# TensorE's lead of a few first-table steps behind each search of the expert layer, and the order of the first loads for the second table

## The chip, the cores and the metric

The kernel runs on one core of a Trainium2 chip. The metric is the device time of one execution in microseconds. Times in the rows are counted from the start of the profiled span.

## What is computed

The reference runs a two-layer latent/context transformer block and then a second block on 256 tokens of width 1024. The change lies in the expert ("PEER") layer, which is called for 512 tokens in layer 0 (latent and context tokens together) and for 256 tokens in layer 1. Cut to what matters:

```python
def peer(h, w_pq, sub_keys, u_tab, v_tab):
    q = (h @ w_pq).reshape(B, T, 8, 2, 64)
    s = einsum('bthcd,hckd->bthck', q, sub_keys)          # 128 keys per half
    top_s, top_i = top_k(s, 16)
    best_s, best_j = top_k(top_s[..., 0, :, None] + top_s[..., 1, None, :], 16)
    expert = i1 * 128 + i2                                 # one of 16384
    w = softmax(best_s)
    act = gelu(einsum('cd,ced->ce', h, u_tab[expert]))
    return einsum('ce,ced->cd', act * w, v_tab[expert])
```

## The kernel before

The two tables U and V (16384 x 1024 each) are not gathered for most tokens. They are run through densely, in 128 tiles `a` of 128 experts. In the **U phase** tile `a` gives gelu(U h) for all dense tokens (`u_product`, L944, three float32r products of high and low halves; in layer 1 some tiles are taken whole, `u_plain`, L919, and layer 1 adds a part sum, `u_sum`, L955). In the **V phase** (L1021 in layer 0, L1046 and L1048 in layer 1) the weighted activations are multiplied with the V tiles. For the first 128 tokens of layer 0 and the first 64 of layer 1, rows of U and V are gathered instead: GpSimd issues one indirect DMA for each of these rows (`u_row`, L2673, `v_row`, L2680), VectorE does the dot product (L2259) and, with V, the sum (L1831).

Beside the U phase runs the **search**, token block by token block (`t`, 128 tokens): TensorE makes four score groups (L982, `rt`), VectorE finds the best 16 of each (`choose`, L2111 and behind it) and ends with the weights of the block (`ww`, an L1823 on `area`). TensorE then transposes indices and weights (L644, `ti`), ScalarE copies them (L1618), VectorE and ScalarE build one-hot matrices for four tokens at a time (a **quad**; ScalarE's part is L1599 and L1604), TensorE multiplies them (L1000, `ow`), ScalarE copies the result (L1635), and GpSimd stores 16 tokens of it to `w_scratch` (L2753). The stored weights of 8 tiles at a time come back with `load_w` (L2763), the activations, stored by `store_g` (L2712), with `load_g` (L2775). Both are multiplied on VectorE (`weigh`) before the V product. VectorE's program has every gathered U row ahead of the first `weigh`.

The order around this is written by hand. Each engine has a generator `early()` that yields five times for each U tile, and calls `fill(n)` to go n **steps** on. On TensorE four steps of a tile hold a quarter of the products and the fifth holds none; a step with products is 6 matmuls of 384 columns in layer 0, 4 pairs in layer 1 (less in a plain tile). ScalarE makes the high half of tile a+2 (layer 0) or a+3 (layer 1) in a tile's first step (`high`, L1265); VectorE makes the low half in the fifth (`low`, an L1823 on `fr`); during the first part of layer 0's searches GpSimd makes the low half instead (L2695). `FILLS` holds the numbers: for layer 0 6 steps behind each score group, 10 for each half of the second selection, 14 for each third of the rest, 3 behind a quad; for layer 1 14, 25, 24 and 4. Counted so, layer 0's searches of t = 1, 2, 3 end at steps 144, 326 and 508 of 640, layer 1's of t = 0, 1 at steps 154 and 396. The block t = 0 of layer 0 is gathered whole and has no quads.

## Time and profile before

| | us |
|---|---|
| median of 3 runs | 3246.27 |
| lowest and highest of them | 3245.52, 3247.68 |
| the profiled execution, its own time | 3238.48 |
| its span | 3236.4 |
| layer 0: U phase about | 394 to 1064 |
| layer 0: V phase about | 1068 to 1592 |
| layer 1: U phase about | 1850 to 2265 |
| layer 1: V phase about | 2266 to 2560 |

TensorE is busy for 3009.5 us of the span (93%), VectorE for 2451.3 (76%), ScalarE for 1536.5 (47%), GpSimd for 942.6 (29%). In a row of the timeline the number in brackets is the idle time of the engine just ahead, and behind the arrow stands what ended it.

### The profile page before, as it was taken

To read this page: it belongs to the slowest core of one execution; us is meant where nothing else is said; L and a number is where in the kernel's file an instruction comes from. 1 tells how busy PE (TensorE), PEld (TensorE's weight loads), DVE (VectorE), ACT (ScalarE), POOL (GpSimd) and SP (SyncE) were. 2 spreads that over 40 slices of the span, in tenths; PEclk is the share of its full clock that TensorE was granted. 3 is DMA by queue.
4 is the path that set the end of the run, shared out by engine and by line. 5 is a ranking of instruction groups with operands and counts; after the bars stand their busy time and mean duration, and the time that the engine had idled before them with its cause. 6 is when DMAs were issued, how large, how long until landed. Compare 5 with 4: busy or idle time off the path is not lost.

```text
span 3236.4 us, 49042 instructions
## 1 busy us (share of the span) xinstructions
PE 3009.5 (93%) x19164; PEld 2657.7 (82%) x19164; DVE 2451.3 (76%) x4976; ACT 1536.5 (47%) x2895; POOL 942.6 (29%) x835
## 2 busy tenths in 40 slices
PE   6998999999999999999979899899999999988898
PEld 4656799989999888888765899888998899755898
DVE  2696588897888688888758678897999866668654
ACT  3455335737557333333444547496555543232543
POOL 0000046565656344344000024454685200000000
PEclk9999999999999999999998999999999999967899
DMA  7384347969789999999527568899999867501444
GB/s 233 97 283 157 127 159 273 341 242 315 271 286 339 370 371 353 381 357 368 174 96 256 182 227 315 278 351 361 380 400 400 325 207 247 158 33 47 155 142 132
DMA packets 352934, 824.41 MB, mean 255 GB/s; under 512 B 20256, under 2 KB 216384, under 8 KB 332608
## 3 DMA queue, kind: packets, MB, share of 16 engines
q1 hardware_dynamic: 257216, 469.79, 41.8%
q0 software_dynamic: 93120, 347.17, 29.3%
q10 hardware_dynamic: 2368, 4.32, 0.4%
q8 instruction: 152, 2.49, 0.3%
q14 instruction: 78, 0.64, 0.1%
HBM read 747.76 MB, written 73.40 MB: 254 GB/s over the span
## 4 chain that ended last, share of the span: by engine, by line
PE 65%; DVE 22%; DMA 6%; ACT 4%; issue 2%; POOL 1%; DVEq 0%; SPq 0%; ACTq 0%; POOLq 0%
PE ps L1021 16%; PE ps L944 16%; PE ps L639 13%; DVE fr L1823 5%; DVE area L1831 4%; DVE area L1823 3%; DMA ring<-in_peer_v 3%; PE ps L1000 3%; PE ps L1109 2%; PE ps L717 2%; PE ps L1101 2%; PE ps L873 2%; DVE plain L2259 1%; ACT fr L1265 1%; PE ps L919 1%
## 5 line engine op out<-in xcount | busy, mean ns | idle before, releaser
L1823 DVE TENSOR_TENSOR fr<-ring,fr 128x1024 fp32r<-128x1024 f32 x641 | 781.7, 1222 | 473.3 <-ACT fr L1265 470.5
L1265 ACT CAST fr<-ring 128x1024 fp32r<-128x1024 f32 x677 | 703.7, 1045 | 566.5 <-PE ps L1021 323.5
L944 PE MATMUL ps<-fr 128*128 128x384 f32 (+1 forms) x4784 | 851.0, 331 | 14.2 <-DVE fr L1823 14.1
L944 PEld LDWEIGHTS ps<-fr 128*128 128x128 f32 x4784 | 789.2, 191 | 19.5 <-DVE fr L1823 17.1
L1021 PE MATMUL ps<-fr 128*128 128x512 f32 x2304 | 523.9, 390 | 4.4 <-DVE fr L1823 4.4
L1021 PEld LDWEIGHTS ps<-fr 128*128 128x128 f32 x2304 | 433.4, 188 | 94.8 <-ACT area L1582 4.7
L639 PE MATMUL ps<-fr 128*128 128x256 f32 (+1 forms) x2928 | 415.3, 304 | 26.2 <-DVE fr L1823 26.2
L639 PEld LDWEIGHTS ps<-fr 128*128 128x128 f32 x2928 | 389.1, 193 | 52.3 <-DVE fr L1823 32.5
L2680 POOL DMA_INDIRECT plain<-in_peer_v,area x192 | 284.9, 1484 | 259.6 <-DVE area L1831 167.0
L1046 PE MATMUL ps<-fr 128*128 128x384 f32 x1024 | 297.6, 362 | 12.9 <-DVE fr L1823 12.4
L2712 POOL DMA_DIRECT2D g_scratch<-area x224 | 127.0, 567 | 581.1 <-ACT area L1582 540.9
L1048 PE MATMUL ps<-fr 128*128 128x192 f32 x1024 | 256.4, 250 | 0.0
L1831 DVE SCALAR_TENSOR_TENSOR area<-plain,area 128x1024 f32<-128x1024 f32 x190 | 243.1, 1279 | 1.0
L1582 ACT ACTIVATE area<-ps 128x384 f32<-128x384 f32 (+1 forms) x256 | 105.7, 413 | 278.8 <-PE ps L944 235.5
L2673 POOL DMA_INDIRECT plain<-in_peer_u,area x128 | 196.1, 1532 | 120.4 <-DVE plain L2259 97.9
L1046 PEld LDWEIGHTS ps<-fr 128*128 128x128 f32 x1024 | 192.1, 188 | 20.9 <-DVE fr L1823 19.9
L2695 POOL TENSOR_TENSOR fr<-ring,fr 128x1024 fp32r<-128x1024 f32 x36 | 91.4, 2539 | 392.0 <-ACT fr L1265 391.6
L1048 PEld LDWEIGHTS ps<-fr 128*128 128x128 f32 x1024 | 195.5, 191 | 0.0
L1823 DVE TENSOR_TENSOR area<-area 128x384 f32<-128x384 f32 (+9 forms) x391 | 183.5, 478 | 7.6 <-DMA area<-w_scratch 5.3
L2259 DVE SCALAR_TENSOR_TENSOR plain<-plain,area 128x1024 f32<-128x1024 f32 x128 | 157.6, 1237 | 15.8 <-DMA plain<-in_peer_u,area 15.8
L1000 PE MATMUL ps<-area 128*128 128x128 f32 x1152 | 154.1, 277 | 10.9 <-DVE area L1828 5.0
L1545 ACT CAST fr<-area 128x384 fp32r<-128x384 f32 (+1 forms) x256 | 110.0, 430 | 107.6 <-DVE area L1823 107.2
(228 smaller groups left out, 3990.5 us busy)
## 6 DMA issues: line engine op xcount, KB each, us to landing
ring<-in_peer_uT SPq DMA_DIRECT2D x128, 1024.0 KB, 6.2
ring<-in_peer_v SPq DMA_DIRECT2D x128, 1024.0 KB, 10.0
ring<-in_w_mod SPq DMA_DIRECT2D x48, 1024.0 KB, 5.3
w_scratch<-acc POOLq DMA_DIRECT2D x36, 1024.0 KB, 8.4
g_scratch<-area POOLq DMA_DIRECT2D x128, 192.0 KB, 5.2
area<-g_scratch POOLq DMA_DIRECT2D x64, 384.0 KB, 8.8
area<-w_scratch POOLq DMA_DIRECT2D x16, 1536.0 KB, 10.0
ring<-in_w_ada SPq DMA_DIRECT2D x24, 1024.0 KB, 5.1
```

The source lines that it names most:

```text
L639: ins = e.matmul(o, lhs, rhs, start=(n == 0), stop=(n == len(pairs) - 1))
L944: ins = e.matmul(o[:, 0:width], pairs[m][0], pairs[m][1], start=(m == 0), stop=(l == 0 and m == last), skip_group_check=l == 1)
L1000: ins = e.matmul(o[:, 128 * j:128 * j + 128], b.OH[:, half, 0, j, :], b.OH[:, half, 1, j, :], start=True, stop=True)
L1021: ins = e.matmul(M.PS[2 * tb + half][:, :], x[:, r, 128 * tb:128 * tb + 128], v[:, c, 512 * half:512 * half + 512], start=(a == 0 and (r, ...
L1046: e.matmul(M.PS[m][:, b.first:T + D], v[:, 0, 128 * m:128 * m + 128], x[:, :, 0:D], start=(a == 0), stop=False, skip_group_check=True)
L1048: ins = e.matmul(M.PS[m][:, b.first:T], v[:, 1, 128 * m:128 * m + 128], x[:, 0, 0:D], start=False, stop=False, skip_group_check=True)
L1265: e.copy(hi, x).then_inc(act.after(("high", name)), 1)
L1823: return e.tensor_tensor(o, a, b, op).then_inc(dve.after(*labels), 1)
L1831: return e.scalar_tensor_tensor(out=o, in0=a, scalar=s, in1=b, op0=op0, op1=op1).then_inc(dve.after(*labels), 1)
L2259: e.scalar_tensor_tensor(out=x, in0=x, scalar=1.0, in1=b.hx, op0=M_, op1=M_, accum_out=b.dot[:, k:k + 1]).then_inc(dve.after(("urow", l, k ...
L2673: e.indirect_dma_start(b.u_rows[k % U_ROWS], None, A[f"peer_u{l}"], bass.IndirectOffsetOnAxis(ap=b.idx[:, k:k + 1], axis=0)).then_inc(M.u_ ...
L2680: e.indirect_dma_start(b.v_rows[k % n], None, A[f"peer_v{l}"], bass.IndirectOffsetOnAxis(ap=b.idx[:, k:k + 1], axis=0)).then_inc(M.v_row_i ...
```

## The change

On TensorE, once a search with quads behind it has been covered, four more U steps are issued ahead of the wait for the weights and the transposes (`early_steps`); the next search takes four fewer behind its first score group. ScalarE does the same with three steps, in layer 1 alone. VectorE's and GpSimd's step counts stay as they are. On GpSimd the first `load_w` moves five steps up in layer 0, ahead of one gather and one store; in layer 1 the first `load_g` moves five steps down instead, and `load_w` stays at its step. The second `load_w` goes behind the second `load_g` and five more steps. The first gathers of V rows, eight and six at once before, go out one by one, one for each tile of the V phase.

```diff
+AHEAD_STEPS = {"pe": (4, 4), "act": (0, 3)}
...
-        quad = 0
+        quad = early_steps = 0
...
-                fill(fill_a)
+                fill(fill_a - (early_steps if h4 == 0 else 0))
...
+            early_steps = AHEAD_STEPS["pe"][l]
+            fill(early_steps)
             w.wait_ge(dve, ("ww", l, t))
...
-            fill(4 * fill_a + 2 * fill_b)
+            fill(4 * fill_a + 2 * fill_b - early_steps)
...
+            early_steps = AHEAD_STEPS["act"][l]
+            fill(early_steps)
             w.wait_ge(pe, ("ti", l, t))
...
-        fill(5)
+        fill(5 + 5 * l)
         w.wait_ge(pe, ("ow", l, D // 4 - 1))
         w.wait_ge(dve, ("oh", l, D // 4 - 1))
         load_g(KEPT[l] // 2 + 0)
-        fill(5)
         for i in range(2):
             w.wait_ge(M.w_stored[i], ("w", l, nst - 2 + i))
         load_w(0)
+        fill(5)
+        load_g(KEPT[l] // 2 + 1)
+        fill(5)
+        load_w(1)
         fill(3)
-        load_g(KEPT[l] // 2 + 1)
-        load_w(1)
-        fill(5)
         load_g(KEPT[l] // 2 + 2)
         load_g(KEPT[l] // 2 + 3)
...
-        for k in range(len(b.v_rows)):
-            v_row(k)
+        v_row(0)
         for a in range(128):
+            if a + 1 < len(b.v_rows):
+                v_row(a + 1)
```

TensorE at the end of layer 0's search of t = 1, before (the rows on `con,area` are the transposes of indices and weights):

```order
L944 MATMUL ps7<-fr 128x384 [waits act_done,dve_done]
L944 MATMUL ps7<-fr 128x384 x23
L644 MATMUL ps0<-con,area 128x128 [waits act_done,dve_done]
L644 MATMUL ps0<-con,area 128x128 x2
L944 MATMUL ps1<-fr 128x384 [waits act_done]
```

The same place in the changed kernel:

```order
L946 MATMUL ps6<-fr 128x384 x23
L946 MATMUL ps7<-fr 128x384 [waits act_done,dve_done]
L946 MATMUL ps7<-fr 128x384 x17
L646 MATMUL ps0<-con,area 128x128 [waits act_done,dve_done]
L646 MATMUL ps0<-con,area 128x128 x2
L946 MATMUL ps7<-fr 128x384 x6
```

Eighteen matmuls of the next tile, three steps with products and one empty one, now stand ahead of the transposes.

TensorE at the start of layer 0's search of t = 3, before (the rows on `area` are score groups):

```order
L982 MATMUL ps0<-area 128x128 x4
L944 MATMUL ps7<-fr 128x384 x18
L944 MATMUL ps1<-fr 128x384 [waits dve_done]
L944 MATMUL ps1<-fr 128x384 x11
L982 MATMUL ps2<-area 128x128 x4
```

And in the changed kernel:

```order
L984 MATMUL ps0<-area 128x128 x4
L946 MATMUL ps1<-fr 128x384 [waits dve_done]
L946 MATMUL ps1<-fr 128x384 x11
L984 MATMUL ps2<-area 128x128 x4
```

Between the first and the second score group 12 matmuls are left of 30.

GpSimd at the end of layer 0's U phase, before, from its last store of expert weights on:

```order
L2753 DMA w_scratch<-acc 128x16x128 [waits act_done]
L2673 DMA plain<-in_peer_u,area 128x1024 [waits dve_done]
L2673 DMA area<-in_peer_u,area 128x1024 [waits dve_done]
L2712 DMA g_scratch<-area 128x384 [waits act_done]
L2775 DMA area<-g_scratch 128x2x384 [waits g_stored1,g_stored0,pe_done]
L2673 DMA area<-in_peer_u,area 128x1024 [waits dve_done]
L2712 DMA g_scratch<-area 128x384 [waits act_done]
L2763 DMA area<-w_scratch 128x3072 [waits w_stored1,w_stored0]
```

And in the changed kernel, from the same store on:

```order
L2759 DMA w_scratch<-acc 128x16x128 [waits act_done]
L2679 DMA plain<-in_peer_u,area 128x1024 [waits dve_done]
L2679 DMA area<-in_peer_u,area 128x1024 [waits dve_done]
L2718 DMA g_scratch<-area 128x384 [waits act_done]
L2781 DMA area<-g_scratch 128x2x384 [waits g_stored1,g_stored0,pe_done]
L2769 DMA area<-w_scratch 128x3072 [waits w_stored1,w_stored0]
L2679 DMA area<-in_peer_u,area 128x1024 [waits dve_done]
L2718 DMA g_scratch<-area 128x384 [waits act_done]
```

The load of the first weights has gone ahead of the last gathered U row and of one store.

## Rows read from the trace of the kernel before

**Rows 1.** Page, part 4: chain that ended last, by engine.

```profile
PE 65%; DVE 22%; DMA 6%; ACT 4%; issue 2%; POOL 1%; DVEq 0%; SPq 0%; ACTq 0%; POOLq 0%
```

**Rows 2.** Waits of TensorE, 395 to 1070: us in total, times, longest.

```profile
PE ps L644 <- DVE area L1823: 12.0, 3, 5.4
```

**Rows 3.** Timeline of TensorE, layer 0: start, us, line, count, idle ahead.

```profile
529.29 0.90 PE L644 MATMUL ps<-con,area 128*128 128x128 f32 x3 [3.28 <-DVE area L1823]
529.84 14.14 PE L944 MATMUL ps<-fr 128*128 128x384 f32 x66
...
718.16 1.32 PE L944 MATMUL ps<-fr 128*128 128x384 f32 x6 [1.61 <-DVE fr L1823]
724.86 0.90 PE L644 MATMUL ps<-con,area 128*128 128x128 f32 x3 [5.37 <-DVE area L1823]
...
741.12 1.13 PE L1000 MATMUL ps<-area 128*128 128x128 f32 x8 [2.02 <-DVE plain L2259]
...
914.17 3.42 PE L944 MATMUL ps<-fr 128*128 128x384 f32 x18 [1.48 <-DVE fr L1823]
920.98 0.90 PE L644 MATMUL ps<-con,area 128*128 128x128 f32 x3 [3.39 <-DVE area L1823]
921.53 12.98 PE L944 MATMUL ps<-fr 128*128 128x384 f32 x66
935.40 1.13 PE L1000 MATMUL ps<-area 128*128 128x128 f32 x8 [0.88 <-ACT area L1604]
```

**Rows 4.** Windows: us, busy of PE, PEld, DVE, ACT, POOL, PEclk, DMA share, GB/s.

```profile
530.00:534.00 4.00, 4.00 (x14) 4.00 (x14) 3.28 (x5) 1.97 (x4) 3.31 (x3) 0.50 0.80 199
```

**Rows 5.** Timeline of VectorE, first selection of layer 0's searches.

```profile
654.90 3.12 DVE L1823 TENSOR_TENSOR fr<-ring,fr 128x1024 fp32r<-128x1024 f32 x1
...
672.53 0.89 DVE L2111 MAX8 area<-ps 128x8 f32<-128x128 f32 x4 [0.69 <-PE ps L982]
...
870.86 0.89 DVE L2111 MAX8 area<-ps 128x8 f32<-128x128 f32 x4 [1.66 <-PE ps L982]
```

**Rows 6.** Timeline of GpSimd beside the first of these.

```profile
654.52 2.42 POOL L2695 TENSOR_TENSOR fr<-ring,fr 128x1024 fp32r<-128x1024 f32 x1
```

**Rows 7.** Timeline of TensorE, layer 0's last U products and first V product.

```profile
1042.62 21.05 PE L944 MATMUL ps<-fr 128*128 128x384 f32 x120
1068.05 7.12 PE L1021 MATMUL ps<-fr 128*128 128x512 f32 x24 [4.37 <-DVE fr L1823]
```

**Rows 8.** Timeline of GpSimd there: last store, last gather, first weights' load.

```profile
1043.78 1.21 POOL L2753 DMA_DIRECT2D w_scratch<-acc  x1 [0.40 <-ACT acc L1635]
...
1050.21 1.55 POOL L2673 DMA_INDIRECT area<-in_peer_u,area  x1 [0.30 <-issue]
...
1052.61 0.55 POOL L2763 DMA_DIRECT2D area<-w_scratch  x1
```

**Rows 9.** Timeline of VectorE there: last gathered U row, first weigh.

```profile
1059.20 1.22 DVE L2259 SCALAR_TENSOR_TENSOR area<-area 128x1024 f32<-128x1024 f32 x1 [1.49 <-DMA area<-in_peer_u,area]
...
1065.74 0.56 DVE L1823 TENSOR_TENSOR area<-area 128x384 f32<-128x384 f32 x1 [5.30 <-DMA area<-w_scratch]
```

**Rows 10.** Timeline of TensorE, layer 1: ends of both searches, first quads, a part sum.

```profile
1939.05 0.55 PE L644 MATMUL ps<-con,area 128*128 128x128 f32 x3 [2.54 <-DVE area L1823]
...
2096.49 0.90 PE L644 MATMUL ps<-con,area 128*128 128x128 f32 x3 [7.02 <-DVE area L1823]
...
2113.09 1.13 PE L1000 MATMUL ps<-area 128*128 128x128 f32 x8 [1.86 <-ACT area L1604]
...
2133.88 0.35 PE L955 MATMUL ps<-area_r 128*128 128x192 f32 x1 [0.35 <-ACT area_r L1566]
```

**Rows 11.** Timeline of VectorE, layer 1, t = 1: the last score group.

```profile
2028.41 0.89 DVE L2111 MAX8 area<-ps 128x8 f32<-128x128 f32 x4 [3.02 <-PE ps L982]
```

**Rows 12.** Timeline of GpSimd, layer 1: first weights' load.

```profile
2223.86 0.60 POOL L2763 DMA_DIRECT2D area<-w_scratch  x1 [7.18 <-DMA w_scratch<-acc]
```

**Rows 13.** Windows, layer 1, tail of the U phase and first V tiles.

```profile
2165.00:2360.00 195.00, 186.65 (x1300) 182.66 (x1301) 173.72 (x272) 127.69 (x248) 114.36 (x67) 0.99 0.98 371
```

More of the change, by code:

```diff
@@ L1605, in one_hot @@
                     act.after(("oh", l, quad)), 1)
-        quad = 0
+        quad = early_steps = 0
         for t in range(T // 128):
-            fill(4 * fill_a + 2 * fill_b)
+            fill(4 * fill_a + 2 * fill_b - early_steps)
             w.wait_ge(dve, ("wsub", l, t))
```

## The prediction

> **What bounds the kernel now.** I read the page first: by the chain that ended last the kernel is TensorE for 65% and VectorE for 22% [rows 1]. Then the waits of TensorE over layer 0's U phase: almost all that it waits there stands ahead of the transposes at the ends of the searches, 12.0 us in three waits, for an instruction of VectorE [rows 2]. The timeline puts them: 3.28 us at t = 1, 1.61 + 5.37 at t = 2, 1.48 + 3.39 at t = 3 [rows 3]. So a search lasts as long as VectorE's selection, and from the transposes to the next search TensorE is without a gap, except for the first quad of a block (2.02 and 0.88 us) [rows 3]. Layer 1 has the same picture, with 2.54 and 7.02 us, and 1.86 us at a first quad [rows 10].
>
> The idle time has a price behind it. In 530 to 534, right behind the first wait, the granted clock is 0.50 (1.2 GHz) [rows 4]; 66 matmuls take 14.14 us there and 12.98 us behind the search of t = 3 [rows 3], where the last 120 of the phase take 21.05, 0.175 each [rows 7], so that 66 would take 11.6.
>
> **A trap first.** Four steps ahead of a wait don't shorten anything by themselves: they are taken from the next search, at whose end TensorE idles again. Search time is VectorE's; the stretch from transposes to next search keeps its number of products. What can be gained is (a) time that VectorE waits for TensorE within a search, (b) slow clock behind the idle time, (c) the waits at first quads, where ScalarE starts its one-hots only once TensorE has finished the tile.
>
> **Layer 0, t = 1.** Four steps are 18 matmuls, 3.16 us, into a wait of 3.28 [rows 3]; their low halves stand ahead of `ww` in VectorE's program, since TensorE uses a tile six steps after VectorE's turn for it. The transposes keep their time. The idle time is gone, and with it the slow clock: 14.14 - 11.6 = **-2.6**. Bounds: 0 if the clock falls all the same, -2.6. I take -2.6, since nothing is left to wait for.
>
> **t = 2.** The second to fourth score groups come 18 matmuls (3.1 us) earlier. VectorE waited for the last one for only 0.69 us [rows 5], so the search gets **-0.6**. The first quad's 2.02 us [rows 3] go: with four steps ahead the tile that ScalarE waits for is finished long before, **-2.0**. The idle time of the search, 6.98 less 0.6, stays but falls apart: VectorE's last low halves come every 6 us against 4.2 us of products for a tile, so about 2 us stand ahead of each of the last two tiles and 2.5 ahead of the transposes. Whether the clock falls then is open: between 0 and the 1.4 to 2.6 us that it costs at the other two searches. I take half, **-1.1**.
>
> **t = 3.** VectorE waits 1.66 us for each of three score groups (one of three like rows [rows 5]), 4.98 in all; they come 18 matmuls earlier, so the search is shortened by **-3.1**. The first quad's wait goes, **-0.9** [rows 3]. Idle time falls from 4.87 to about 1.7, so the slow clock goes: 12.98 - 11.6 = **-1.4**. By the count of steps one more with products falls ahead of the last quad, **+1.0**. Sum of layer 0 up to its last quad: -10.7.
>
> **Between quads.** The low half of a tile now sometimes stands behind the one-hots of the same quad on VectorE, where TensorE waited for nothing of its own. There the half is ready about 2 us before TensorE gets to it by my count of steps, so 0. Bounds: -1 and the rival below.
>
> **From the last quad to V.** This is a chain: product, copy, store, load of the weights, `weigh`, ScalarE's and VectorE's halves. It takes from 1042.6 to 1068.05, and 21.05 us of U products lie beside it [rows 7]. Four steps fewer are left, so products cover only 16.8 of it: of what the lead wins at t = 3's end nothing is won here, and TensorE idles about 9 us. The load moves up: at most from 1052.61 to where the gather was issued, 1050.21, so -2.4 [rows 8]. But the last gathered row goes behind it. Before, that row had landed by 1059.2 and the weights (1.5 MB) by 1065.7 [rows 9], 6.5 us later in one queue where landings kept the order of issue. Turned round, the row comes last, near 1065.1 (one store fewer is ahead), then 1.22 us of VectorE for it, then `weigh` at 1066.3 instead of 1065.74: **+0.5**. Bounds -2.4 (the row isn't held up) and +2. I take the queue's order, since both rows are from it. The longer idle time makes the V phase start slow for longer: its first 24 products took 7.12 us [rows 7], some 1.5 more than 0.175 x 512/384 each gives; I add **+0.7**, bounds 0 and +2. V rows one by one, and the second weights later, cost nothing: they are due six and eight V tiles on, 4 us each. Layer 0: -10.7 + 0.5 + 0.7 = -9.5.
>
> **Layer 1.** At t = 0 the transposes keep their time, 2 us of products go into 2.54 [rows 10], and the slow clock was not there; nothing. The search of t = 1 starts three steps with products shorter, 1.8 us; VectorE waited longer than that for the last score group (3.02 [rows 11]), and its later waits for high halves move with TensorE: **-1.8**. First quad of t = 1: of 1.86 us 0.2 is left, since ScalarE is one step behind TensorE instead of level: **-1.7**; at t = 0 the part sum then waits on ScalarE, **+0.4**. The 7.02 us become about 5, and the slow clock behind them stays. Between quads the three engines are nearly level; one part sum in four waited 0.35 [rows 10], now two will, within what VectorE leaves idle: 0, bounds -3 and +3.5. GpSimd's 7.18 us wait for the last store [rows 12] stands at the same step and holds the same gathers; the V phase starts a fixed time after the last quad. Of -3.1 I take four fifths, **-2.5**, since DMA is at 0.98 there [rows 13].
>
> **The sum.** -9.5 - 2.5 = -12.0. Against that the whole search meets GpSimd's low halves elsewhere: one low half on VectorE took 3.12 us [rows 5] beside a subtraction on GpSimd that ran until 656.94 [rows 6], against 1.22 for the others. There are a handful of such meetings in each search, some 2 us each; they can fall either way, and I add 1. That is -11.0: the profiled execution's 3238.5 would be 3227.5, and as the median of the runs lies 7.8 above that execution, 3246.3 - 11 = **3235**.
>
> The Trainium skill (SBUF — State Buffer, section "Who interferes with whom") says that a VectorE instruction with two inputs in SBUF and a GpSimd instruction that reads SBUF don't share: the later one is fully blocked. By that rule the trace agrees (3.12 ends 1.1 us after the subtraction's end). It speaks against counting the 3.1 us at t = 3 as safe, and is the third rival.
>
> **The rivals.**
> 1. *Nothing but the first quads.* VectorE's selection turns out to be paced by its own work, and the clock falls behind the scattered idle time as before. For it: TensorE's idle time only changes place. Against it: three waits of 1.66 on score groups. Left are -2.9 and -1.3 at first quads and -0.6 in the search of t = 2, with +1.2 at the V start: -3.6, **3242**. Chance 0.25.
> 2. *Slower: low halves behind the one-hots.* With TensorE four steps on, a low half issued behind a quad's one-hots comes too late once in every five quads. It decides if VectorE, held by a gathered row, is more than about 2 us late there. Such a wait was 1.48 to 1.61 at search ends [rows 3]; 19 times in layer 0 and 10 in layer 1 at 0.8 is +23, less 11: **3258**. For it: VectorE's rows wait for gathers near the end. Against it: no such wait in the quads before. Chance 0.1.
> 3. *Collisions.* One or two more blocked instructions in each of the three searches, 2 us each, +6 on the forecast: **3241**. Chance 0.15.
> 4. *More.* The last gathered row isn't held up by the weights, and the clock stays up at t = 2: -2.9 and -1.1, **3231**. Chance 0.15.
>
> The forecast itself has 0.35.
>
> **How the numbers follow.** A measurement tells 0.2% here, 6.5 us, so faster is below 3239.8. The forecast is nearly all in that, the fourth rival too, the third by a third; the first is within. Faster 0.54, same 0.35, slower 0.11 (the second rival and a little of the third). The range takes the forecast, the first, third and fourth rivals with their bounds: 3228 to 3247.
>
> **What would show it.** In the changed profile: the wait at the first transposes under 0.5 us and PEclk at 1.00 behind it; score groups of t = 3 without waits of 1.66 on VectorE and that search 3 us shorter; no waits at first quads of layer 0; an idle TensorE of about 9 us ahead of the first V product, with a gathered row, not the weights, as the last thing that VectorE waits for. Waits of TensorE for an L1823 on `fr` within the quads, or a V start more than 28 us after the last quad, would prove me wrong.

## The result, and the profile after

| | before | after |
|---|---|---|
| median of 7 runs, us | 3244.16 | 3224.98 |
| lowest and highest | 3236.31, 3247.68 | 3215.46, 3229.71 |
| ratio, with 95% interval | | 0.9949 (0.9938 to 0.9961) |
| span of the profiled execution | 3236.4 | 3222.9 |

The change makes the kernel 0.5% faster: by the ratio 16.5 us, with an interval from 12.7 to 20.1. The forecast was 11 us and 3235; the time lies below its range, which began at 3228. Of all executions of all kernels below, one of six_steps' ten took 4776.6 us at a mean granted clock of 0.56, where the other nine had 0.93 to 0.96; it is left out of its ratio.

Line numbers of TensorE's part are two to four higher in the changed kernel (L944 is L946, L644 is L646, L982 is L984, L1000 is L1004, L1021 is L1025, L955 is L957), those of ScalarE four to six (L1566 is L1570, L1604 is L1608, L1635 is L1641), those of VectorE and GpSimd six (L1823 is L1829, L2111 is L2117, L2673 is L2679).

First the timeline of TensorE in layer 0, the rows that answer to [rows 3] (start, us, line, count, in brackets the idle time just ahead and what ended it):

```profile
532.18 0.55 PE L646 MATMUL ps<-con,area 128*128 128x128 f32 x3 [0.16 <-DVE area L1829]
532.48 11.71 PE L946 MATMUL ps<-fr 128*128 128x384 f32 x66
544.04 1.05 PE L1004 MATMUL ps<-area 128*128 128x128 f32 x8
...
716.38 4.46 PE L946 MATMUL ps<-fr 128*128 128x384 f32 x24 [1.61 <-DVE fr L1829]
723.08 0.55 PE L646 MATMUL ps<-con,area 128*128 128x128 f32 x3 [2.24 <-DVE area L1829]
723.38 12.75 PE L946 MATMUL ps<-fr 128*128 128x384 f32 x72
735.97 1.05 PE L1004 MATMUL ps<-area 128*128 128x128 f32 x8
...
909.56 2.37 PE L946 MATMUL ps<-fr 128*128 128x384 f32 x12 [0.36 <-DVE fr L1829]
911.77 0.49 PE L646 MATMUL ps<-con,area 128*128 128x128 f32 x3
...
915.00 9.64 PE L946 MATMUL ps<-fr 128*128 128x384 f32 x54 [0.65 <-DVE fr L1829]
```

Of 3.28, 5.37 and 3.39 us ahead of the three transposes 0.16, 2.24 and nothing are left, and the waits at the first quads (2.02 and 0.88) are gone. New is a wait of 0.65 us for a low half between the transposes and the first quad of t = 3. The slow clock behind the first wait is gone too: 66 products take 11.71 us where they took 14.14. The windows behind the three transposes and behind layer 0's V start say so (column by column: busy time of PE, PEld, DVE, ACT, POOL, then the granted clock, the DMA share and GB/s):

```profile
532.50:536.50 4.00, 4.00 (x26) 4.00 (x24) 3.63 (x5) 3.30 (x6) 3.67 (x3) 1.00 0.78 192
723.40:727.40 4.00, 4.00 (x26) 4.00 (x24) 4.00 (x6) 1.98 (x4) 2.66 (x3) 1.00 0.97 292
912.00:916.00 4.00, 3.35 (x21) 3.03 (x20) 4.00 (x6) 3.40 (x6) 2.76 (x2) 1.00 0.52 152
1056.30:1060.30 4.00, 4.00 (x11) 3.13 (x12) 2.34 (x4) 0.79 (x3) 3.10 (x3) 0.57 0.98 392
```

Where [rows 4] had 0.50, the granted clock is 1.00 behind all three searches; only behind the longest idle stretch, ahead of V, it is still at its lower level for most of the window.

Then the way from layer 0's last quad to V, TensorE's rows against [rows 7], GpSimd's (last store, load of the first weights, last gather) against [rows 8], VectorE's against [rows 9]:

```profile
1031.22 12.74 PE L946 MATMUL ps<-fr 128*128 128x384 f32 x72
1045.83 6.03 PE L946 MATMUL ps<-fr 128*128 128x384 f32 x24 [1.87 <-DVE fr L1829]
1056.25 44.04 PE L1025 MATMUL ps<-fr 128*128 128x512 f32 x186 [4.39 <-DVE fr L1829]
```

```profile
1032.39 1.21 POOL L2759 DMA_DIRECT2D w_scratch<-acc  x1 [2.87 <-ACT acc L1641]
...
1040.04 0.57 POOL L2769 DMA_DIRECT2D area<-w_scratch  x1 [1.24 <-DMA w_scratch<-acc]
1040.91 0.99 POOL L2679 DMA_INDIRECT area<-in_peer_u,area  x1 [0.30 <-issue]
```

```profile
1052.79 1.23 DVE L2265 SCALAR_TENSOR_TENSOR area<-area 128x1024 f32<-128x1024 f32 x1 [5.88 <-DMA area<-in_peer_u,area]
1053.94 0.08 DVE L2265 DVE_READ_ACCUMULATOR area<-area 128x1 f32 x1
1053.94 0.55 DVE L1829 TENSOR_TENSOR area<-area 128x384 f32<-128x384 f32 x1
```

The last thing that VectorE waits for is now a gathered row, which was issued 0.87 us behind the load and landed 11.9 us after its issue (before, ahead of the load, 9.0 us). `weigh` follows with no wait for the weights. TensorE stands idle for 6.3 us ahead of V (1.87 and 4.39), not for the 9 that the prediction named as a sign: the last 24 products take 6.03 us at a granted clock of 0.72, where 24 take 4.2 at 1.00.

On VectorE the two rows that answer to [rows 5], the low half beside GpSimd's subtraction and the one wait for a score group that is left of t = 3's three:

```profile
655.01 2.57 DVE L1829 TENSOR_TENSOR fr<-ring,fr 128x1024 fp32r<-128x1024 f32 x1
```

```profile
861.46 0.89 DVE L2117 MAX8 area<-ps 128x8 f32<-128x128 f32 x4 [1.66 <-PE ps L984]
```

Between the quads of layer 0 TensorE waits for nothing; before, one quad of t = 3 had waited for a one-hot of VectorE:

```profile
990.75 1.16 PE L1000 MATMUL ps<-area 128*128 128x128 f32 x8 [1.17 <-DVE area L1828]
```

In layer 1 the transposes at 2081.71 wait 2.62 us and the products ahead of them 2.12, where 7.02 stood [rows 10]. But between the quads of t = 1 there are more waits than before. The waits of TensorE and of ScalarE there, first of the kernel before (2113 to 2209), then of the changed one (2098 to 2197); columns: us in total, times, longest:

```profile
PE ps L1000 <- DVE area L1828: 2.6, 6, 0.4
PE ps L955 <- ACT area_r L1566: 2.0, 6, 0.3
...
ACT acc L1635 <- PE ps L1000: 1.1, 6, 0.2
```

```profile
PE ps L957 <- ACT area_r L1570: 6.2, 12, 0.7
...
ACT acc L1641 <- PE ps L1004: 4.6, 12, 0.6
```

**All stages at once.** From the timeline of TensorE the start of each stage's first matmul can be read; the stages between them are in this table, in us, with two of the experiments below beside them. Within layer 0's U phase up to the last quad, stages with the same program repeat from kernel to kernel within 0.15 us, but for the quads of t = 3 (105.9 to 106.7 in the nine kernels with four steps). Other stages scatter more: the first row takes 392.3 to 401.2 us over all fourteen profiles, the stretch from layer 1's last quad to V 53.8 to 58.8. So a difference of a microsecond in the former can be read from a single profile, where the medians tell 4.

| stage | before | after | l0_only | act_level |
|---|---|---|---|---|
| start to first score group, layer 0 | 392.26 | 395.19 | 397.57 | 397.38 |
| to transposes t = 1 | 137.03 | 136.99 | 137.02 | 137.01 |
| to first quad | 14.54 | 11.86 | 11.85 | 11.86 |
| quads, to search t = 2 | 109.07 | 108.97 | 108.98 | 108.97 |
| search t = 2 | 71.96 | 70.07 | 70.07 | 70.09 |
| to first quad | 16.26 | 12.89 | 12.89 | 12.89 |
| quads, to search t = 3 | 109.07 | 107.93 | 107.94 | 107.93 |
| search t = 3 | 70.79 | 67.87 | 67.88 | 67.86 |
| to first quad | 14.42 | 12.71 | 12.71 | 12.73 |
| quads, to the last one | 106.41 | 105.93 | 105.91 | 106.26 |
| last quad to V | 26.24 | 25.84 | 27.97 | 24.78 |
| V phase, projections of layer 1 | 782.29 | 779.63 | 779.13 | 783.91 |
| layer 1: search t = 0 | 88.71 | 88.81 | 89.48 | 88.79 |
| to first quad | 13.86 | 13.88 | 15.05 | 13.80 |
| quads of t = 0 | 49.31 | 50.72 | 49.32 | 48.08 |
| search t = 1 | 94.27 | 92.42 | 94.27 | 92.42 |
| to first quad | 16.60 | 16.22 | 16.50 | 17.14 |
| quads of t = 1 | 96.12 | 98.48 | 96.22 | 93.98 |
| last quad to V | 57.15 | 57.28 | 54.36 | 53.92 |
| V start to the end | 970.04 | 969.21 | 969.28 | 972.00 |

Layer 0 from its first score group to V is 14.7 us shorter (675.79 and 661.06), layer 1 from its first score group to V 1.8 us longer (416.02 and 417.81). The 2.9 us at the top, where the program is the same, and the 2.7 of the "V phase, projections" row are within such scatter and not shown to be work of the change. The granted clock differs there: in a stretch of layer 1's first projections it is 0.63 before (1604 to 1622) and 0.81 after (1592 to 1610).

### The profile page after: what moved, and what is told of

It is laid out like the page before. It is cut to its first block, busy times and chain, and to the rows that moved or that the text cites. A ratio compares the mean times of both kernels' runs of the same rounds, so it can differ in the third digit from the quotient of the medians.

```text
span 3222.9 us, 48984 instructions
## 1 busy us (share of the span) xinstructions
PE 3010.5 (93%) x19164; PEld 2659.3 (83%) x19164; DVE 2447.6 (76%) x4976; ACT 1533.6 (48%) x2895; POOL 960.5 (30%) x835
## 4 chain that ended last, share of the span: by engine, by line
PE 67%; DVE 21%; DMA 5%; ACT 4%; issue 2%; POOL 1%; DVEq 0%; SPq 0%; POOLq 0%; ACTq 0%
PE ps L946 16%; PE ps L1025 16%; PE ps L641 14%; DVE fr L1829 5%; DVE area L1837 4%; PE ps L1004 3%; DVE area L1829 3%; DMA ring<-in_peer_v 3%; PE ps L719 2%; PE ps L1113 2%; PE ps L1105 2%; PE ps L875 2%; ACT fr L1269 1%; PE ps L921 1%; DVE acc L1829 1%
## 5 line engine op out<-in xcount | busy, mean ns | idle before, releaser
L1829 DVE TENSOR_TENSOR fr<-ring,fr 128x1024 fp32r<-128x1024 f32 x641 | 779.8, 1219 | 458.6 <-ACT fr L1269 454.8
L946 PE MATMUL ps<-fr 128*128 128x384 f32 (+1 forms) x4784 | 851.5, 331 | 19.8 <-DVE fr L1829 19.8
L946 PEld LDWEIGHTS ps<-fr 128*128 128x128 f32 x4784 | 787.9, 191 | 26.3 <-DVE fr L1829 24.2
L1025 PE MATMUL ps<-fr 128*128 128x512 f32 x2304 | 524.1, 390 | 4.4 <-DVE fr L1829 4.4
L1025 PEld LDWEIGHTS ps<-fr 128*128 128x128 f32 x2304 | 433.5, 188 | 94.9 <-ACT area L1586 4.7
L2686 POOL DMA_INDIRECT plain<-in_peer_v,area x192 | 299.7, 1561 | 251.9 <-DVE area L1837 170.1
L2679 POOL DMA_INDIRECT plain<-in_peer_u,area x128 | 194.3, 1518 | 124.2 <-DVE plain L2265 104.7
L1829 DVE TENSOR_TENSOR area<-area 128x384 f32<-128x384 f32 (+9 forms) x391 | 182.7, 475 | 5.6 <-DMA area<-g_scratch 3.8
L1004 PE MATMUL ps<-area 128*128 128x128 f32 x1152 | 152.8, 275 | 2.0 <-ACT area L1608 2.0
```

The costliest lines, as they stand in the source:

```text
L946: ins = e.matmul(o[:, 0:width], pairs[m][0], pairs[m][1], start=(m == 0), stop=(l == 0 and m == last), skip_group_check=l == 1)
L1004: ins = e.matmul(o[:, 128 * j:128 * j + 128], b.OH[:, half, 0, j, :], b.OH[:, half, 1, j, :], start=True, stop=True)
L1025: ins = e.matmul(M.PS[2 * tb + half][:, :], x[:, r, 128 * tb:128 * tb + 128], v[:, c, 512 * half:512 * half + 512], start=(a == 0 and (r, ...
L1829: return e.tensor_tensor(o, a, b, op).then_inc(dve.after(*labels), 1)
L2679: e.indirect_dma_start(b.u_rows[k % U_ROWS], None, A[f"peer_u{l}"], bass.IndirectOffsetOnAxis(ap=b.idx[:, k:k + 1], axis=0)).then_inc(M.u_ ...
L2686: e.indirect_dma_start(b.v_rows[k % n], None, A[f"peer_v{l}"], bass.IndirectOffsetOnAxis(ap=b.idx[:, k:k + 1], axis=0)).then_inc(M.v_row_i ...
```

## The experiments

Two questions stand: is the gain all layer 0's, and why does layer 1 lose what its shorter search wins? The times are compared with runs of the kernel before on the same chip. All kernels take the changed kernel and alter the numbers of `AHEAD_STEPS` or GpSimd's order.

### Which part of the change does what

**l0_only**: the steps ahead in layer 0 alone.

```diff
-AHEAD_STEPS = {"pe": (4, 4), "act": (0, 3)}
+AHEAD_STEPS = {"pe": (4, 0), "act": (0, 0)}
```

> Four steps ahead in layer 0 alone (the pair of numbers (4, 0) for TensorE, (0, 0) for ScalarE), GpSimd's new order in both layers. Theory A (from comparing the two traces by stages: layer 0's U phase is 14.7 us shorter, layer 1 from its first score group to its V start is 1.8 us longer): this kernel is 2 us faster than the changed one, 18 to 21 us faster than the kernel before, and its stretches between quads in layer 1 are 49.3 and 96.1 us again, as in the kernel before. Theory B (as forecast: both layers gain, 2.5 us of it in layer 1): it is 2 to 3 us slower than the changed one, and the search of t = 1 in layer 1 lasts 94.3 us again while the stretches between quads don't change.

Measured: 3226.5 us, ratio 0.9950 (0.9936 to 0.9965), which is 16.2 us. The quads of layer 1 are back at 49.32 and 96.22 us, the search of t = 1 at 94.27. Layer 0 gives the same 14.3 us up to its last quad. As a time of the whole it can't be told from the change, and A's 18 to 21 us are not reached. By its stages A's mechanism holds: from the first quad of t = 0 in layer 1 to the last one of t = 1 it takes 256.3 us, as before, against 257.8. But layer 0's V starts 27.97 us after the last quad against 25.84, with the same program: there the gathered row landed 14.0 us after its issue in place of 11.9.

**l1_only**: the steps ahead in layer 1 alone.

```diff
-AHEAD_STEPS = {"pe": (4, 4), "act": (0, 3)}
+AHEAD_STEPS = {"pe": (0, 4), "act": (0, 3)}
```

> Steps ahead in layer 1 alone ((0, 4) for TensorE, (0, 3) for ScalarE), GpSimd's new order in both layers. Theory A: the search of t = 1 in layer 1 is 1.9 us shorter and the stretches between quads are 1.4 and 2.4 us longer; with nothing from layer 0 the time is that of the kernel before or up to 3 us more. Theory B: 2.5 to 4 us faster than the kernel before, since the longer stretches between quads in the changed kernel's profile were chance.

Measured: 3244.0 us, ratio 1.0008 (0.9997 to 1.0018): nothing won. The search of t = 1 is 92.50 us, the quads are 50.83 and 98.34. The longer quads of the changed kernel were no chance. Theory B, at least 2.5 us faster, falls: the interval ends at 1.0 us faster.

**gpsimd_only**: no steps ahead, GpSimd's new order alone.

```diff
-AHEAD_STEPS = {"pe": (4, 4), "act": (0, 3)}
+AHEAD_STEPS = {"pe": (0, 0), "act": (0, 0)}
```

> No steps ahead in either layer, only GpSimd's new order (the first two weight loads moved, V rows issued one by one). Theory A (the weights load earlier but the last gathered row is held up behind them, so nothing is won): within 1 us of the kernel before; V starts 25 to 26 us after the last quad of layer 0, and the last thing VectorE waits for there is a gathered row. Theory B (the order on GpSimd is where the unexpected part of the gain came from, since the changed kernel won 8 us more than forecast by the medians): 3 to 8 us faster than the kernel before, with the gain in a V phase or at its start.

Measured: 3245.8 us, ratio 1.0009 (1.0000 to 1.0018). No gain, so theory B falls; by the ratio it is 2.9 us slower (0 to 5.8), where A had at most 1. From layer 0's last quad to V it took 28.76 us, 2.5 more than before and beyond what theory A gave, since the gathered row came 15.2 us after its issue (14.6 in l1_only). VectorE's row for it:

```profile
1074.29 1.22 DVE L2265 SCALAR_TENSOR_TENSOR area<-area 128x1024 f32<-128x1024 f32 x1 [8.71 <-DMA area<-in_peer_u,area]
```

In layer 1 the same order made the way from the last quad to V 53.77 us instead of 57.15, so that in these two profiles the two nearly cancel (but see order_by_layer for the second).

**tensor_only**: the steps ahead with GpSimd's old order.

```diff
-        fill(5 + 5 * l)
+        fill(5)
...
         load_g(KEPT[l] // 2 + 0)
+        fill(5)
         for i in range(2):
             w.wait_ge(M.w_stored[i], ("w", l, nst - 2 + i))
         load_w(0)
-        fill(5)
-        load_g(KEPT[l] // 2 + 1)
-        fill(5)
-        load_w(1)
         fill(3)
+        load_g(KEPT[l] // 2 + 1)
+        load_w(1)
+        fill(5)
...
-        v_row(0)
+        for k in range(len(b.v_rows)):
+            v_row(k)
         for a in range(128):
-            if a + 1 < len(b.v_rows):
-                v_row(a + 1)
```

> The steps ahead as in the change, (4, 4) and (0, 3), with GpSimd's order as in the kernel before. Theory A: as fast as the changed kernel within 1.5 us (16 to 19 us faster than the kernel before); at the last quad of layer 0 the weights are what VectorE waits for last, 1 to 2 us after the row has come, and V starts 24.5 to 26 us after the last quad. Theory B: 3 to 8 us slower than the changed kernel, because the steps alone give what was forecast for them.

Measured: 3221.4 us, ratio 0.9942 (0.9927 to 0.9957). The whole gain is there without GpSimd's part, and V starts 24.76 us after the last quad. The gather of the last row and the load behind it on GpSimd, then what VectorE waits for:

```profile
1039.09 1.00 POOL L2679 DMA_INDIRECT area<-in_peer_u,area  x1 [0.30 <-issue]
1040.67 0.55 POOL L2769 DMA_DIRECT2D area<-w_scratch  x1
```

```profile
1047.70 1.23 DVE L2265 SCALAR_TENSOR_TENSOR area<-area 128x1024 f32<-128x1024 f32 x1 [0.51 <-DMA area<-in_peer_u,area]
1052.86 0.56 DVE L1829 TENSOR_TENSOR area<-area 128x384 f32<-128x384 f32 x1 [3.92 <-DMA area<-w_scratch]
```

With the row first, it lands 8.6 us after its issue, and the weights, loaded 0.6 us later than in the changed kernel, are weighed 1.1 us sooner (1052.86 against 1053.94). A had the time, the V start and the weights as the last wait right; the row came 5.2 us ahead of the weights, not 1 to 2.

**order_by_layer**: steps in layer 0 alone; GpSimd's old order of the first loads in layer 0, the new one in layer 1, as `if l == 0:` with the old lines and `else:` with the new ones. The V rows still go out one by one.

> Four steps ahead in layer 0, none in layer 1; GpSimd's order as in the kernel before in layer 0 and as in the change in layer 1. Theory A (the gain is layer 0's steps, 14.3 us up to its last quad in every profile that has them; GpSimd's new order costs 1 to 2.5 us at layer 0's V start and wins about 3 us from layer 1's last quad to its V start): the stretch from the last quad to V in layer 0 is 24.8 us, in layer 1 53.8 to 54.4 us, and the kernel is 17 to 21 us faster than before, 1 to 4 us faster than the changed one. Theory B (the differences of GpSimd's order are chance of landings): layer 1's stretch is 55.9 to 57.2 us again and the time is the changed kernel's.

Measured: 3222.2 us, ratio 0.9945 (0.9927 to 0.9963), within A's 17 to 21 us at 17.8. Layer 0's stretch from last quad to V was 24.73, as A had it. Layer 1's was 56.11, theory B's value, which A had at 53.8 to 54.4: over all the profiles with GpSimd's new order in layer 1 that stretch took 53.8 to 58.8 us, with the old one 57.15 (before) and 55.87 (tensor_only). So the 3 us that I read from two profiles are not shown; the stretch hangs on something that differs between executions.

### Why layer 1 loses between its quads

In the changed kernel ScalarE is three steps ahead and TensorE four, so that ScalarE stands one step further behind than before. The next four kernels alter these numbers in layer 1; all have GpSimd's order by layer, as order_by_layer.

**act_level**: as order_by_layer, with both engines four steps ahead in layer 1:

```diff
-AHEAD_STEPS = {"pe": (4, 0), "act": (0, 0)}
+AHEAD_STEPS = {"pe": (4, 4), "act": (0, 4)}
```

> Four steps ahead in both layers, and four for ScalarE in layer 1 in place of three, so that ScalarE stands to TensorE between quads as it did before; GpSimd's order by layer as in order_by_layer. Theory A (ScalarE is the busiest engine between quads in layer 1; being one step further behind TensorE it and TensorE wait for each other, 0.7 us per part sum): layer 1's stretches between quads fall from 50.8 and 98.4 to about 48.7 and 95 us, with the search of t = 1 still 92.4: 2 to 3 us faster than order_by_layer. Theory B (the stretches are longer because VectorE or the transfers fall behind when TensorE is ahead): they stay at 50.8 and 98.4 us, and the kernel is 2 us slower than order_by_layer.

**act_two**: (4, 4) and (0, 2).

> As act_level, (4, 4) for TensorE, but two steps ahead for ScalarE in layer 1 in place of four. Theory A (each step that ScalarE stands further behind TensorE costs in layer 1 between quads: with four there the stretches are 48.1 and 94.0 us, with three 50.8 and 98.4): with two they are 51 to 54 and 100 to 104 us. Theory B (three steps were only an unlucky meeting of the two orders, and the distance as such costs nothing): with two they are 48 to 49 and 94 to 96 us.

**act_five**: (4, 4) and (0, 5).

> As act_level, but five steps ahead for ScalarE in layer 1 in place of four: ScalarE is one step nearer to TensorE than in the kernel before. Theory A (the nearer the better, until ScalarE waits for products): the waits of TensorE for part sums fall from 0.7 us, the stretches between quads are 47 to 48 and 92.5 to 94 us, and the kernel is as fast as act_level or 1 to 2 us faster. Theory B (level is the optimum, since a cast of a step that TensorE has not done holds up the one-hots behind it): they are 49 to 51 and 95 to 98 us, and the kernel is 2 to 4 us slower than act_level.

**three_l1**: (4, 3) and (0, 3).

> Three steps ahead in layer 1 on both TensorE and ScalarE, else as act_level. Theory A (what matters is that both have the same number): the stretches between quads are 48 to 49 and 94 to 95 us, the search of t = 1 is 92.4 to 93.5 us. Theory B (what matters is that TensorE and ScalarE meet at certain steps, and three is a bad number for ScalarE): they are 50 to 51 and 97 to 99 us, as with (4, 3).

Measured for the four:

| TensorE's, ScalarE's steps in layer 1 | quads t = 0 | quads t = 1 | search t = 1 | time, ratio |
|---|---|---|---|---|
| 0, 0 (order_by_layer) | 49.34 | 96.12 | 94.31 | 3222.2, 0.9945 |
| 4, 2 (act_two) | 54.64 | 107.27 | 92.49 | 3240.4, one run |
| 4, 3 (the change) | 50.72 | 98.48 | 92.42 | 3225.0, 0.9949 |
| 4, 4 (act_level) | 48.08 | 93.98 | 92.42 | 3215.7, 0.9919 (0.9901 to 0.9937) |
| 4, 5 (act_five) | 48.94 | 93.60 | 92.49 | 3225.1, 0.9931 (0.9908 to 0.9954) |
| 3, 3 (three_l1) | 49.38 | 93.75 | 93.04 | 3222.2, one run |

Theory A had the direction each time and the size too small: 48.7 and 95 us for act_level, at most 54 and 104 for act_two. The distance of ScalarE behind TensorE sets the price: from level to one step behind 2.6 and 4.5 us, one more step another 3.9 and 8.8. Level with three steps gives what level with four gives at t = 1, so it isn't the number three. Level with four is also shorter than level with none, by 1.3 and 2.1 us. Why isn't tested; VectorE's waits for ScalarE's high halves between the quads of t = 1 go the same way, 1.3 us in all against 6.7 in order_by_layer (7.2 in the changed kernel, 14.9 in act_two). The waits between the quads of t = 1, of act_level (2103 to 2197) and of act_two (2105 to 2213):

```profile
ACT acc L1641 <- PE ps L1004: 1.3, 1, 1.3
...
PE ps L957 <- ACT area_r L1570: 4.0, 6, 0.7
```

```profile
PE ps L957 <- ACT area_r L1570: 13.5, 19, 1.3
...
ACT acc L1641 <- PE ps L1004: 12.9, 24, 0.8
```

Read with the two programs, and with the sizes in the table, it is a wait in both directions: TensorE's part sum waits for ScalarE's cast (L1570), which stands one step late in ScalarE's program, and ScalarE's copy (L1641) then waits for the quad's products (L1004), which stand behind that part sum in TensorE's. Each such pair is time in which ScalarE, the busiest engine here, does nothing. The windows of the stretch, of the kernel before, the changed one and act_level:

```profile
2113.09:2209.21 96.12, 91.48 (x673) 88.14 (x674) 89.28 (x164) 94.20 (x229) 49.69 (x43) 1.00 0.96 351
```

```profile
2097.93:2196.41 98.48, 91.89 (x670) 87.50 (x670) 91.28 (x167) 93.07 (x229) 47.23 (x43) 1.00 0.96 347
```

```profile
2103.00:2197.00 94.00, 89.66 (x672) 87.56 (x671) 91.41 (x165) 92.23 (x228) 48.97 (x43) 1.00 0.98 358
```

ScalarE is busy for 94.20 of 96.12, for 93.07 of 98.48, and for 92.23 of 94.00 us. By the ratios act_level is about 8 us faster than order_by_layer, with intervals that overlap; by the stages from layer 1's first quad to its last it is 4.8 (251.6 against 256.4), where A had 2 to 3. Five steps for ScalarE give nothing more between the quads than four (142.54 us in the two stretches against 142.06), nor do they cost what B had there. By its ratio act_five is 4 us slower than act_level, and the intervals overlap widely, so the time doesn't decide between the two theories.

### How far ahead

**two_steps** and **six_steps**: as order_by_layer, with two and with six steps in layer 0. **seven_l1**: as act_level, with seven steps on both engines in layer 1.

```diff
-AHEAD_STEPS = {"pe": (4, 0), "act": (0, 0)}
+AHEAD_STEPS = {"pe": (2, 0), "act": (0, 0)}
```

> Two steps ahead in layer 0 in place of four, else as order_by_layer. Theory A (idle time of 1.5 to 2 us or more ahead of the transposes lets the clock fall, and part of the waits is left): at t = 1 the wait is 1.2 to 3.3 us and the stretch from the transposes to the first quad is 14.5 us, as without steps; up to the last quad 6 to 9 us are won of the 14.3. Theory B (the slow clock comes of long waits alone): that stretch is 11.9 us, and 11 us or more are won.

Measured: 3228.0 us in one run; 11.15 us are won up to the last quad of layer 0, theory B's side. TensorE's rows at the ends of the three searches:

```profile
531.68 0.55 PE L646 MATMUL ps<-con,area 128*128 128x128 f32 x3 [2.23 <-DVE area L1829]
531.98 11.69 PE L946 MATMUL ps<-fr 128*128 128x384 f32 x66
...
723.39 0.55 PE L646 MATMUL ps<-con,area 128*128 128x128 f32 x3 [3.30 <-DVE area L1829]
723.70 11.72 PE L946 MATMUL ps<-fr 128*128 128x384 f32 x66
...
906.33 4.46 PE L946 MATMUL ps<-fr 128*128 128x384 f32 x24 [1.48 <-DVE fr L1829]
913.14 0.90 PE L646 MATMUL ps<-con,area 128*128 128x128 f32 x3 [2.35 <-DVE area L1829]
913.69 14.00 PE L946 MATMUL ps<-fr 128*128 128x384 f32 x72
```

Behind a wait of 2.23 us and behind one of 3.30 the clock stays up (66 products in 11.7 us). Behind 1.48 and 2.35 us it is at its lower level, 0.50 from 913 to 916, and 1.00 from 916.5 on (72 in 14.00). So neither theory has the clock right: a wait of 3.30 us passed without it and one of 2.35 did not. Two steps out of four already bring back 11 of the 14.3 us, because a full clock at t = 1 and t = 2 is won by both.

> Six steps ahead in layer 0 in place of four, else as order_by_layer. Theory A (the search of t = 3 still holds about 1.9 us of waits of VectorE for score groups, that of t = 2 3.8 us of waits of TensorE; at t = 1 nothing is left): t = 1 loses up to 2 us at the transposes and has them back in the next search; t = 3's search is 1 to 2 us shorter; all in all 0 to 2 us faster than order_by_layer. Theory B (the transposes are then late for the first quad of each block, or VectorE's low halves fall behind): 2 to 5 us slower, with waits at the first quads or within the quads of layer 0.

Measured: 3236.2 us, ratio 0.9981 (0.9968 to 0.9994): 12 us slower than with four by the ratios (8.1 up to layer 0's last quad by the stages), more than B gave, and at another place. The search of t = 2 takes 77.39 us instead of 70.07. Its first rows on VectorE, and GpSimd's beside them:

```profile
655.71 0.89 DVE L2117 MAX8 area<-ps 128x8 f32<-128x128 f32 x4 [3.98 <-PE ps L984]
656.52 5.81 DVE L1829 TENSOR_TENSOR fr<-ring,fr 128x1024 fp32r<-128x1024 f32 x1
```

```profile
656.02 2.35 POOL L2701 TENSOR_TENSOR fr<-ring,fr 128x1024 fp32r<-128x1024 f32 x1
658.30 0.56 POOL L2718 DMA_DIRECT2D g_scratch<-area  x1
658.88 2.35 POOL L2701 TENSOR_TENSOR fr<-ring,fr 128x1024 fp32r<-128x1024 f32 x1
```

A low half on VectorE that takes 1.22 us elsewhere takes 5.81: it begins inside one of GpSimd's subtractions and ends 1.1 us after the end of the second (661.23). It is the low half that TensorE, now six steps on, needs next, and TensorE stands still for 6.16 us:

```profile
662.38 8.13 PE L946 MATMUL ps<-fr 128*128 128x384 f32 x30 [6.16 <-DVE fr L1829]
```

The 30 products behind it take 8.13 us in place of 5.49 in order_by_layer, and the granted clock of 658 to 669 is 0.54. With four steps (order_by_layer) the wait at this place is 1.14 us. This is the third rival's mechanism: it decides at six steps and not at four; five weren't run. The last products of that search wait for low halves as well, 1.59 and 1.50 us, and the transposes stand behind them.

> Seven steps ahead in layer 1 on both engines, else as act_level. In act_level TensorE still waits 2.1 and 5.2 us at the end of layer 1's search of t = 1. Theory A (the remaining idle time takes three more steps): the wait ahead of the transposes falls from 5.2 to about 2.5 us, and the kernel is 1 to 3 us faster than act_level. Theory B (as with six in layer 0, the products at the search's end then stand ahead of the transposes and wait for low halves that VectorE has not done): the searches of layer 1 are 2 us or more longer and the kernel is 2 to 8 us slower.

Measured: 3224.3 us, ratio 0.9934 (0.9918 to 0.9951). The wait ahead of the transposes of t = 1 is gone and that search is 0.6 us shorter (91.87), so A was right that the wait shrinks; it had 2.5 us left. B's longer searches are not there. But from the transposes to the first quad it takes 19.60 us instead of 17.14, and the quads take 50.00 and 95.54: the part sums behind the transposes wait 1.82 and 1.14 us for ScalarE. Over layer 1 it is 7.5 us longer than act_level (415.65 and 408.13), at a place that neither theory named.

## Why the prediction was too small

Three steps of it failed. Layer 0's terms add up to -9.5, and the profiles show -14.7. Layer 1's term "between quads ... 0" was +1.4 and +2.4. And the 7.8 us that were added because "the median of the runs lies 7.8 above that execution" were not there in the changed kernel.

Point by point, as the prediction's steps have them; forecast and measurement in us.

| step | forecast | measured |
|---|---|---|
| layer 0, t = 1: idle time filled, clock up | -2.6 | -2.7 |
| t = 2: search | -0.6 | -1.9 |
| t = 2: first quad and clock | -3.1 | -3.4, with 6 products more in it |
| t = 2: quads | 0 | -1.1 |
| t = 3: search | -3.1 | -2.9 |
| t = 3: first quad and clock | -2.3 | -1.7 |
| t = 3: quads | +1.0 | -0.5, with 6 products more and a wait of 1.17 gone |
| last quad to V, V start | +1.2 | -0.4 |
| layer 0 | -9.5 | -14.7, with 0.1 in the quads of t = 1 |
| layer 1: search t = 0, its first quad | +0.4 | +0.1 |
| quads of t = 0 | 0 | +1.4 |
| search t = 1 | -1.8 | -1.9 |
| its first quad | -1.7 | -0.4, with 4 products more |
| quads of t = 1 | 0 | +2.4 |
| last quad to V | 0 | +0.1 |
| layer 1 (forecast at four fifths) | -2.5 | +1.8 |

**Layer 0.** The mechanisms held at nearly every place: the transposes of t = 1 stand where they stood, TensorE's clock stays at 1.00 behind the searches, the first quads don't wait, VectorE's waits of 1.66 us for score groups fell from three to one, and that search is 2.9 us shorter. Four terms were mis-sized. *The clock at t = 2* was taken at half; it stayed up, also with two steps, and 66 products fell from 13.68 to about 11.7 us. *The search of t = 2*: VectorE's work on the fourth score group begins 1.12 us sooner in the search, by the 0.69 us of the wait and by a low half that a subtraction of GpSimd held up for less (2.57 us in place of 3.12). The other 0.8 is a conversion behind it (L2148, now L2154): it took 1.50 us from 677.40 and now 0.73 from 676.39, in both kernels ending 0.15 us behind the end of a subtraction of GpSimd (678.76, 676.97). I had put +1 on such meetings over the whole; here they fell the other way, and with six steps they cost far more. *Products ahead of the last quad*: the step more is there, 450 weight loads of products between t = 3's quads against 444, worth the +1.0. But I had written that TensorE has no gap between the transposes and the next search but for first quads, and so missed the wait of 1.17 us at 990.75 shown above. It is there in the profiles of before, l1_only and gpsimd_only, and gone in the changed one; the stretch became 0.5 us shorter. At t = 2 6 products moved from between the quads to ahead of the first one, which only shifts 1.1 us from one row to the other. The new wait of 0.65 us ahead of t = 3's first quad is why -1.7 stands there and not -2.3. *The last quad to V*: the chain came out as forecast, with the gathered row last and `weigh` behind it, but `weigh` begins 23.5 us after the last quad against 23.9 before, where I had +0.5. The longer slow start that I added for 0.7 us is small at most: the granted clock of V's first four microseconds is 0.57 against 0.63 before (1068.1 to 1072.1).

**Layer 1.** The forecast gain of 2.5 us was a loss of 1.8. The step that failed is "between quads the three engines are nearly level ... 0, bounds -3 and +3.5". I had seen that ScalarE is one step behind TensorE instead of level, and even put 0.4 us on it once, but took the quads at zero, by what VectorE leaves idle. VectorE isn't the engine that counts there. [rows 13] show ScalarE at 127.7 of 195 us, but over a window that reaches from the quads far into the V phase; the window on the quads alone, above, shows it at 94.2 of 96.1. An engine with 2% of slack has none to give a wait to.

**The time as a whole.** For the profiled execution the forecast was 3227.5, and it took 3225.0, 13.5 us less than before. Of that -12.9 lie in the two U phases by the stages, -0.8 between layer 1's V start and the end, and +2.9 and -2.7 in stretches that scatter by as much. So 2.5 of the 10 us that the forecast missed by are those of the kernel. The other 7.8 are the median's distance from the profiled execution, read from three runs: over seven runs of the kernel before it is 5.7, in the changed kernel 0.0, and in the experiments with four runs or more it lies between -8.1 (act_level) and +3.7 (gpsimd_only). It tells which execution was profiled, nothing of the kernel, and carrying it over put 3235 where 3227.5 had been worked out. That 3227.5 came so close was luck: layer 0 won 5.2 us more than its terms and layer 1 4.3 less. Between the 13.5 of the profiles and the 16.5 (12.7 to 20.1) of the ratio nothing need be explained.

**The rivals.** The first (only first quads) was wrong, since searches and clock both moved. The second (low halves behind the one-hots, slower) did not happen with four steps: no product between layer 0's quads waits for a low half. The third (collisions) cost no time with four, though the low half of 2.57 us kept TensorE waiting for 1.14 within the search of t = 2, and did with six. The fourth is half right: the clock stayed up at t = 2, while the row was held up. And none of them had ScalarE. The measured time lies below what each of them gave; the offset of 7.8 us is in all of these times.

**A better version.** act_level, four steps on both engines in layer 1 and GpSimd's old order in layer 0, has 0.9919 (0.9901 to 0.9937) against 0.9949 (0.9938 to 0.9961) for the change; by the ratios about 26 us less than the kernel before, 10 less than the change, from four runs. Its stages show where: 6.2 us from layer 1's first quad to its last (251.6 against 257.8) and 1.1 at layer 0's V start; another 3.4 from the last quad to V are within the scatter of that stretch. The profiled execution, the slowest of the four, doesn't show the whole: it took 3223.8 us, 1.2 less than that of the change, with 7.1 more in the V phases and projections.

## What to carry to other kernels

Where engines run the same list of steps by hand-written leads, a lead given to one engine has to be given also to an engine that hands it something at the same step and has hardly any idle time, or the difference comes back as a wait in both directions; one step cost up to 9 us in a stretch of a hundred. Where that engine has slack it costs nothing: between the quads of layer 0's t = 3 ScalarE's waits for the quads' products went from 11.0 to 20.9 us without a loss, with ScalarE busy for 82 of 106. Before calling such a distance free, read busy time in a window that holds only that stretch, not one that reaches over its ends. And a lead has an upper end: what the waiting engine needs next must be finished by the other one in its worst meeting, not in its median time. A forecast for one execution should be compared with one execution; the distance of a median from it doesn't carry over.

## What the runs showed of the hardware

**A blocked VectorE instruction can stay blocked over two of GpSimd's.** The low half of 5.81 us in six_steps ran from 656.52 to 662.33, over a subtraction of GpSimd to 658.37, a DMA issue, and a second subtraction from 658.88 to 661.23. In the 0.5 us between the two it didn't get through. In the changed kernel the gap is as long, and there it did: its low half (655.01 to 657.58) ends behind the start of GpSimd's second subtraction, which takes 2.84 us in place of 2.4.

```profile
654.10 2.39 POOL L2701 TENSOR_TENSOR fr<-ring,fr 128x1024 fp32r<-128x1024 f32 x1
656.44 0.56 POOL L2718 DMA_DIRECT2D g_scratch<-area  x1
657.02 2.84 POOL L2701 TENSOR_TENSOR fr<-ring,fr 128x1024 fp32r<-128x1024 f32 x1
```

What decides between the two outcomes the runs don't show. The same pair met for 3.12 us in the kernel before [rows 5, 6]. In all three the low half ends 1.1 us behind the end of the subtraction that held it. The Trainium skill (SBUF — State Buffer, section "Who interferes with whom") says that such instructions contend for an exclusive lock, and that the order of issue decides which one blocks. The traces agree with that for the first subtraction in each of the three, and for the second in the changed kernel. They don't for the second in six_steps: it started 2.36 us after the low half and yet held it, and 5.81 us is beyond what one subtraction of 2.35 explains.

**The length of a wait doesn't tell whether the clock falls.** In this kernel a wait of 3.28 us was followed by a granted clock of 0.50, and one of 3.30 by 1.00; 2.35 us with 1.48 ahead of it by a fall to the lower level, 2.24 with 1.61 ahead of it by none.

**A gathered row behind a load of 1.5 MB.** Ahead of it on GpSimd's queue, the row was there for VectorE 8.2 to 10.1 us after its issue in ten profiles; behind it 11.9, 14.0, 14.6 and 15.2 us in the four that have that order in layer 0.
